# A fused two-layer transformer step in split float32: one accumulator region per tile, low weights in place, splitting two slabs ahead

## The reference, cut to what matters

```python
def rmsnorm(x, g):
    xf = x.astype(jnp.float32)
    xf = xf * lax.rsqrt(jnp.mean(xf * xf, axis=-1, keepdims=True) + EPS)
    return xf.astype(x.dtype) * g
...
    h = rmsnorm(x, pre_g) * (1.0 + scale[:, None]) + shift[:, None]
    proj = h @ w_in
    ...
    merged = g_a * (y_a @ w_br_attn) + g_p * (y_p @ w_br_pool)
    o = merged @ w_out
    return x + gate[:, None] * rmsnorm(o, post_g)
...
def _conv_ffn(h, w_up, conv_w, conv_b, w_down):
    u = h @ w_up
    ...
    gate, val = jnp.split(u, 2, axis=-1)
    return (jax.nn.silu(gate) * val) @ w_down
```

## Time and profile before

| what | value |
|---|---|
| median of 3 runs | 2520.79 us (2519.3 to 2521.08) |
| the profiled execution | 2521.72 us |
| its span, first to last instruction | 2519.9 us |
| mean granted TensorE clock | 0.951 of full |
| products and weight loads | 12836 each |
| device memory traffic | 580.67 MB, 230 GB/s |

### The profile page before, as it was taken

One profiled execution on the slowest core, in us unless ns is written; L12 is line 12 of the kernel. 1 busy time (PEld: TensorE's weight loads), 2 busy tenths in 40 slices (PEclk: granted clock), 3 DMA queues, 4 the chain that ended last, 5 costly groups with the idle time before them and its releaser, 6 DMA issues.

```text
span 2519.9 us, 32064 instructions
## 1 busy us (share of the span) xinstructions
PE 2312.4 (92%) x12836; PEld 1982.0 (79%) x12836; DVE 1789.0 (71%) x2282; ACT 1153.7 (46%) x1637; POOL 94.1 (4%) x113
## 2 busy tenths in 40 slices
PE   2499999999995889999999999997999999989997
PEld 1388888888784768888888888886888888878886
DVE  6767777779854787777677888646777777764444
ACT  1343455555445345454455455445444444434443
POOL 1000000000000000000011100000000000000000
PEclk8599999999996989999999999998999999999998
DMA  9867778878843757578777788743555555556662
GB/s 380 353 229 271 260 260 286 292 269 308 307 158 120 258 175 259 202 248 293 263 262 256 253 291 306 268 167 117 186 198 184 171 197 184 189 158 188 188 184 80
DMA packets 313032, 580.67 MB, mean 230 GB/s; under 512 B 12187, under 2 KB 105167, under 8 KB 308533
## 3 DMA queue, kind: packets, MB, share of 16 engines
q1 hardware_dynamic: 300224, 535.86, 62.3%
q0 software_dynamic: 11328, 40.26, 4.9%
q10 hardware_dynamic: 1332, 2.51, 0.3%
HBM read 557.61 MB, written 20.97 MB: 230 GB/s over the span
## 4 chain that ended last, share of the span: by engine, by line
PE 60%; DVE 9%; ACT 4%; issue 2%; DMA 0%; DVEq 0%; ACTq 0%
PE gemm L1607 38%; PE gemm L1608 19%; DVE w_lo L985 2%; DVE mod_acc L978 1%; PE extra L1430 1%; ACT w_hi L676 1%; ACT quad_work L676 1%; PE extra L1422 1%; DVE proj L1057 1%; ACT scores L676 0%; ACT operand_main L676 0%; DVE small L1198 0%; DVE scores L1195 0%; DVE proj L1054 0%; PE extra L1516 0%
## 5 line engine op out<-in xcount | busy, mean ns | idle before, releaser
L1607 PE MATMUL gemm<-operand_main,w_hi 128*128 128x512 f32 x4880 | 1740.0, 404 | 72.9 <-issue 26.5
L1608 PE MATMUL gemm<-operand_main,w_lo 128*128 128x256 f32 x4880 | 1329.3, 283 | 0.0
L1607 PEld LDWEIGHTS gemm<-operand_main,w_hi 128*128 128x128 f32 x4880 | 911.9, 191 | 281.0 <-issue 44.3
L985 DVE TENSOR_TENSOR w_lo<-w_stage,w_hi 128x1024 fp32r<-128x1024 f32 (+2 forms) x774 | 876.0, 1160 | 361.1 <-ACT w_hi L676 360.6
L676 ACT ACTIVATE w_hi<-w_stage 128x1024 fp32r<-128x1024 f32 (+2 forms) x776 | 766.3, 1007 | 653.5 <-PE gemm L1608 652.4
L1608 PEld LDWEIGHTS gemm<-operand_main,w_lo 128*128 128x128 f32 x4880 | 934.7, 192 | 30.1
L978 DVE SCALAR_TENSOR_TENSOR mod_acc<-mod_stage,c_silu,mod_acc 128x1024 f32<-128x1024 f32 x224 | 285.4, 1315 | 0.6 <-DMA mod_stage<-in_w_mod 0.6
L676 ACT ACTIVATE low_part<-gemm 128x256 f32<-128x256 f32 x329 | 125.4, 384 | 326.7 <-PE gemm L1607 302.6
L1607 PE MATMUL gemm<-ffn_hidden,w_hi 128*128 128x512 f32 x704 | 249.8, 401 | 9.8 <-issue 9.8
L1608 PE MATMUL gemm<-ffn_hidden,w_lo 128*128 128x256 f32 x704 | 196.1, 282 | 0.0
L1607 PEld LDWEIGHTS gemm<-ffn_hidden,w_hi 128*128 128x128 f32 x704 | 132.5, 190 | 41.7 <-issue 10.1
(11 more groups left out here) (198 smaller groups left out, 1214.5 us busy)
## 6 DMA issues: line engine op xcount, KB each, us to landing
w_stage<-in_w_in SPq DMA_DIRECT2D x128, 1024.0 KB, 6.2
mod_stage<-in_w_mod SPq DMA_DIRECT2D x192, 512.0 KB, 5.6
w_stage<-in_w_up SPq DMA_DIRECT2D x88, 1024.0 KB, 5.0
w_stage<-in_w_down SPq DMA_DIRECT2D x64, 704.0 KB, 4.8
w_stage<-in_w_ada SPq DMA_DIRECT2D x32, 1024.0 KB, 8.0
w_stage<-in_w_merge SPq DMA_DIRECT2D x32, 1024.0 KB, 5.5
w_stage<-in_w_out SPq DMA_DIRECT2D x32, 1024.0 KB, 5.5
mod_stage<-in_w_ada SPq DMA_DIRECT2D x32, 512.0 KB, 6.0
```

What stands on the lines that cost most here:

```text
L985: tt(WL[:, s1 % 2, c0:c1], WST[:, s1 % 4, c0:c1], WH[:, s1 % 2, c0:c1].bitcast(F32), ALU.subtract)\
L1607: hi = lambda **kw: mm(bank[:, :], WH[:, s % 2, c0:c0 + P], X_[:, k, :], **kw)
L1608: lo = lambda **kw: mm(bank[:, T:2 * T], WL[:, s % 2, c0:c0 + P], X_[:, k, 0:T], **kw)
```

## The change

- Products: a chunk of a tile is now three products of 256 columns into the same 256 columns of PSUM: hi·xh, hi·xl, lo·xh. A bank holds two tiles; a group of four tiles needs two banks, and consecutive groups alternate between `gemm0/1` and `gemm2/3`.
- Evacuation: one instruction on ScalarE for two tiles (projection, gates, down), or DVE operations that read the bank directly (merges, 512 elements at once; convolution). In up, ScalarE computes the last tap with the bias from the bank, DVE adds the other two from the bank; `conv_in` is gone.
- Buffers: five stage buffers; DVE writes the low part over the stage buffer it comes from; three `w_hi` buffers. ScalarE and DVE split slab s+2 at slab s. A load waits until PE has finished the slab five before it.
- Down: 4 column groups of 4 tiles by 11 slabs of 1 MB, in place of 16 groups of one tile. The last block's hidden work is done in hooks of down's slabs 0 to 2, and PE waits for one hidden block a slab.
- branch2's and qkvb's bodies are written as single phases; in qkvb a head's last step stands ahead of the evacuation. Some one-element ScalarE instructions and the copies `k_head`, `v_head` are gone.

```diff
-        WST = at("w_stage", [P, 4, SLAB], F32, take(32 * KB))
-        WH = at("w_hi", [P, 2, SLAB], F32R, take(16 * KB))
-        WL = at("w_lo", [P, 2, SLAB], F32R, take(16 * KB))
+        o_wst = take(RAW * 8 * KB)
+        WST = at("w_stage", [P, RAW, SLAB], F32, o_wst)
+        WL = at("w_lo", [P, RAW, SLAB], F32R, o_wst)
+        WH = at("w_hi", [P, HIS, SLAB], F32R, take(HIS * 8 * KB))
...
+            def free_slot(t):
...
+                elif t >= MOD0_ROWS + RAW:
+                    sp.wait_ge(slab_used, 2 * (t - MOD0_ROWS - RAW) + 2)
...
+            def split_hi(n):
+                for h, c0, c1 in halves(n):
+                    if h == 0:
+                        act.wait_ge(w_landed[slot_of(n)], landed(n))
+                    positive(act, slab_used, 2 * (n - HIS) + h + 1)
+                    activate(WH[:, n % HIS, c0:c1], WST[:, slot_of(n), c0:c1], ACT.Copy).then_inc(hi_made, 1)
...
+            def evac(g):
+                for u in range(g.banks):
...
+                    wait_bank(act, g, u)
+                    if g.evac == "proj":
+                        t = g.kw["tile"] + 2 * u
+                        activate(PROJ[:, t:t + nt, :], acc, ACT.Copy).then_inc(done, 1)
...
+            def tap(g):
+                positive(act, (ffn_gated, hid_done)[g.kw["half"]], g.kw["b"])
+                for u in range(2):
+                    wait_bank(act, g, u)
+                    for m in (2 * u, 2 * u + 1):
...
+                for s, (g, q) in enumerate(ph.slabs):
+                    if ph.slab0 + s + AHEAD < len(slabs):
+                        split_lo(ph.slab0 + s + AHEAD)
+                    for h in ph.hooks.get(s, ()):
+                        hook(*h)
+                    for r in mods_behind(ph, s):
+                        mod_row(ph, r)
+                    if q == g.slabs - 1 and g.by == "dve":
+                        evac(g)
...
+            def gemm(n):
...
+                        if g.operand == "hid":
+                            pe.wait_ge(hid_done, q + 1)
+                    for m in range(g.tiles):
+                        u = m // 2
+                        if kcs[0] == 0 and q == 0 and m % 2 == 0 and g.gi >= 2:
+                            before = groups[g.gi - 2]
+                            wait_evac(pe, before, min(u + 1, before.banks))
+                        acc = bank_of(g, u)[:, (m % 2) * T:(m % 2 + 1) * T]
+                        for kc in kcs:
...
+                            mm(acc, hi, x_[:, k, 0:T], start=(k == 0 and m % 2 == 0), stop=False, skip_group_check=True)
+                            mm(acc, hi, x_[:, k, T:2 * T], start=False, stop=False, skip_group_check=True)
+                            ins = mm(acc, lo, x_[:, k, 0:T], start=False, stop=(k == nk - 1), skip_group_check=True)
```

More of the change, by code:

```diff
@@ L223, in build @@
         w_in2 = A["w_in_2"][0]
[L226 to L231, removed]
+        phases = []
+        one = lambda c: Group(w_in, c, 4, "main", "proj", tile=c // P)
@@ L236, in build @@
[L236 to L242, removed]
@@ L250, in build @@
-        segs.append(Segment("gk", 1, [Group(w_in2, 5632, 0, 4, "main", "proj", tiles=1, bank0=3, tile=59)],
-                            pre=[("prep_h", 1)], post=[("gla_gate", 0)]))
[L252 to L256, removed]
-                                hooks={**attn_hooks(0, pair[0]), **attn_hooks(4, pair[1])},
-                                late={**attn_late(0, pair[0]), **attn_late(4, pair[1])},
-                                mod=mod, post=[] if kv0 else [("mod_end", 5)]))
@@ new lines, in build @@
+        for i in range(4):
+            last = {0: [("ffn_val", 10)], 1: [("ffn_hi", 10)], 2: [("ffn_lo", 10)]}
+            phases.append(Phase("down", i, [Group(A["w_down_2"][0], 512 * i, 11, "hid", "late", tile=4 * i)],
+                                hooks={} if i else last, post=[("resid", 2)] if i == 3 else []))
+        groups, slabs = [], []
+        n_banks, n_by, mods = 0, {"act": 0, "dve": 0}, 0
+        for ph in phases:
+            ph.slab0 = len(slabs)
+            ph.mod0 = mods
+            mods += 2 * ph.mod[2] if ph.mod else 0
+            for g in ph.groups:
+                g.gi = len(groups)
+                groups.append(g)
+                g.bank0, g.by0 = n_banks, n_by[g.by]
+                n_banks += g.banks - 1
+                n_by[g.by] += g.banks
+            for s, (g, q) in enumerate(ph.slabs):
+                g.last = len(slabs)
+                slabs.append((ph, g, q))
@@ L734, in norm @@
+            gate_no = {}
+            for g in groups:
+                if g.evac == "gate":
+                    gate_no[g.gi] = len(gate_no)
             def norm(k, ready, src, src0):
@@ L781, in stage @@
                     base, x0, o0 = x_tiles(k)
-                    last = sg.tile0 + sg.tiles * sg.bodies
-                    norm(norm_of[("resid", k)], lambda j: act.wait_ge(evac_done, last - 12 + 4 * j), base, o0)
+                    outs = [p.groups[0] for p in named(("out1", "out2", "down")[k])]
+                    norm(norm_of[("resid", k)], lambda j: wait_evac(act, outs[j]), base, o0)
                     if k == 2:
@@ L932, in _ @@
+                for h in ph.late:
+                    hook(*h)
+                for what, k in ph.post:
+                    stage(what, k, ph)
         @block.vector
@@ L1625, in _ @@
-                repeat(pe, sg.bodies, body)
-                for what, k in sg.post:
-                    stage(what, k, sg)
+                for s in range(len(ph.slabs)):
+                    gemm(ph.slab0 + s)
+                    for h in ph.hooks.get(s, ()):
+                        hook(*h)
+                for h in ph.late:
+                    hook(*h)
+                for what, k in ph.post:
+                    stage(what, k, ph)
 _INS = ["x", "c", "rel_bias_table", "w_ada", "b_ada", "pre_norm_g", "post_norm_g", "w_in", "attn_sink", "w_pool_group",
```

855 lines of the change are left out of this document (356 added, 499 removed).

## The result

The changed kernel takes 2538.3 us (median of 5 runs, 2536.45 to 2543.41), the kernel before beside it 2521.1 us (2519.3 to 2526.8): ratio 1.0067, 95% interval 1.0051 to 1.0084. That is 17 us slower. I had forecast 43 us faster, 2478, with a range up to 2520.

A forecast was written before the change was run, and what follows sets the result against it. PE was taken to bound the kernel: 5840 product pairs at 353.4 ns, 2064 us. From 2521.7, less 44.5 of removed waits and 0.9 to the median, came 2476, said as 2478; range 2458 to 2520.

The forecast's parts named there:

- I take the pitch as unchanged, 353 ns: All 5840 chunks: start-to-start time stays 353 ns with three products of 256 columns; ends -12 to +39 us.
- rival 1: Every chunk: the third product has a fixed price, 16.7 ns; pitch 370 ns, +97 us, 2575; chance 0.12.
- Rival 2: Every chunk: all three products take the neighbouring pair's 120 ns; pitch 360 ns, +39 us, 2517; chance 0.12.
- Rival 3: Every chunk: a small fixed price of 2 to 3 ns once; +12 to +17 us, 2492; chance 0.10.
- gates2: Three of four boundaries in this stage: PE's 2.56 us waits for DVE's gate_out go, with the clock after; 10.2 us.
- gk and qkv2: Behind the gk columns: PE's 11.6 us wait for w_lo shrinks, qkv2's first two slabs being split earlier; 9.5 us.
- up's start: Start of the feed-forward: PE's 2.95 us wait for w_lo behind prep_h goes; 2.9 us.
- branch2's start: Start of branch2: PE's 2.04 us wait goes, with 0.8 us of clock; 2.8 us.
- last block and down: Feed-forward, between up and down: PE's 9.79 us wait goes, with 2.3 us of clock after it; 12.1 us together.
- branch merges: Branch1, out1's start and branch2's end: fewer DVE operations per two tiles shorten PE's waits; 4 us together.
- small ones: Waits of 0.56 to 0.84 us at four other boundaries, and residual norms starting 0.42 us earlier; 3 us.
- Case 4: Stages with DMA at 0.85, or gates2 and qkv2: late loads or DVE splits lose half the gain; 2500; chance 0.14.

The follow-up runs named there:

- The two kernels with one order: Kernel before, 512-column product first in a tile's last chunk too; the second also adds the low-part product into alternating bank halves; ratios 0.9953 and 0.9952 on one chip.

## Why the prediction was wrong

**The step that failed first is "I take the pitch as unchanged, 353 ns, because the time goes with the columns in both directions".** It measured 360.0 ns, +38.6 us, the upper end that I had kept (+39), and the kernel before with nothing but the split has the same 360.0. The row for it was there: three equal products of 256 columns are three times the neighbouring pair's 120 ns, and a value from the very shape counts more than a ratio between shapes. I had to take 120.

The reason was also rival 1's, not mine: a product costs 13.3 ns beside its columns. What hid this was that the 512 + 256 pair ran 6.7 ns over the sum of its parts, so the ratio of 0.24 to 0.12 in the order of time looked like columns alone. The 33 ns that rival 1 found lost in a pair are two times 13.3 and these 6.7. Hence its 16.7 ns and its +97 us were too much: a third product adds 13.3 ns, and the 6.7 go. What I held against it, the f32 products of the earlier trace rows, was no row for it: they are of another format and take 0.215 us for 256 columns, where these take 0.120. Rival 2 (120 ns each, 2517, chance 0.12) had the pitch exactly, and missed the total by 21 us for the steps below. Rival 3's 2 to 3 ns a product is too little by 10. The Trainium skill (TensorE: Matmul & The Clock Gate, Back-to-back issue gap) states one column a cycle and 2.5 ns for a warm product, in a formula that leaves the weight loads out. The rate, which I had set aside, agrees with the 0.417 ns a column measured at 2.4 GHz; the fixed part does not, for these products, each behind a weight load of its own: 13.3 ns.

**Left out: the start, +15.8 us.** I wrote of loads only that they are issued in time. Five stage buffers also mean five loads of 1 MB ahead of everything that the other queues bring at the start; that term stood at nothing, without a reason. Giving back one load takes 17 us off by the ratios.

**Left out: the first pair's last attention step ahead of a mod row, +10.7 us.** The change moved it from behind the group to the hooks of the fourth slab. Behind DVE's wait for PE stood a mod row, behind that the next rows' loads and the next pair's scores, for which PE waits. With the order of the two turned, 12 us of the two bodies go.

**Left out: some 5 us in the first block's gate and merge bodies**: 3.4 in the merges, of which 2.5 come with the split of the product alone, and 1.1 in the last gate body, which do not; there the clock was 0.96 in place of 1.00.

**The savings were right, and low.** Term by term, beyond the pitch: gates2 10.2 expected, 11.8 found; gk and qkv2 9.5, 14.3 (qkv2's gap 5.83 us where "about 5" was said); up's start 2.9, 3.8; branch2's start 2.8, 1.2 and then 2.5 at out2's; last block and down 12.1, 12.1 (9.9 + 2.2); branch merges 4, 4.9, with out1's gap 2.69 against 2.6; small ones 3, 3. Sum 44.5 expected, 54 found, with the draw of some 2 us said above in gk's, and 4.5 of gates2's that the split product brings by itself. The evacuation itself was free, as said. Case 4 did not happen at those places; waits of its kind appeared in the attention bodies, which I had not named.

Together: 2521.7 + 38.6 + 15.8 + 10.7 + 5 - 54 = 2537.8, and the profiled execution took 2538.2 (span 2535.8). That the changed kernel with a wide product came out at 2478.0, the number forecast, is chance: its first product starts 18 us late in its profile and its rhythm is mostly 346.7 ns, which no term of the forecast has.

The ranking of chances was the second fault. 0.52 went to the case with no change of pitch, with 0.34 for the three with a longer one, though the only row with the shape in question spoke for these.

## What to carry to other kernels

- Splitting a product bought nothing in columns here and paid a price per product, though TensorE's busy share shows it full either way; price a new shape by the row of that shape, and multiply by the count before anything else (here 6.6 ns x 5840 took back 39 of the 54 us that all the removed waits gave).
- A buffer more is a load more in flight: look at what else is loading at that moment, above all at the start. A step moved ahead on a queue carries its own wait there; ask what stands behind it.
- Keep the parts of a change apart. The waits it removed were worth some 50 us without what the split product brings by itself. With a 512-column product in the same schedule (timing only, its columns overlap) the kernel took 1.8% less than the one before, part of it by the faster rhythm.

## What the runs showed of the hardware

- At full clock a float32r product with its own 128-column weight load took 226.9 ns for 512 columns, 173.5 for 384, 120.1 for 256, and 111.6 ns for 192 and for 128 alike: 13.3 ns + 0.417 ns a column, with a floor.
- Alternating 512 and 256 columns took either 346.7 or 353.4 ns a pair, steadily, changing at pauses with one exception seen. The two kernels with one order, over ten runs each, scatter over 15 to 23 us, the kernel before over 15 in thirty runs; the changed kernel over 7 in five runs, and its variants at 360.0 with ten runs over 5 to 10.
- A product of 512 and one of 128 took 339.7 ns, 226.9 + 112.8: the short one adds the floor's 111.6, within 1.2 ns.
- Six merge bodies of the first block, with attention products between the weight products, took 0.30 us more than the pitch explains when their weight products were split; why is open.
